# Expert weights as units of one expert's matrix in all eight pairs of a layer, instead of in the middle six

## The reference

```python
for e in range(N_EXPERTS):                      # 16
    y = (silu(hf @ w_gate[e]) * (hf @ w_up[e])) @ w_down[e]
    out = out + gates[:, e:e + 1] * y
```

## Time and profile before

| | |
|---|---|
| median of 3 runs | 698.88 us (697.13 to 699.33) |
| the profiled execution's own time | 698.79 us |
| its span from the first to the last instruction | 697.0 us |
| TensorE matmul busy | 659.8 us, 95% |
| TensorE weight load busy | 342.1 us, 49% |
| VectorE, ScalarE, GpSimd busy | 319.6, 167.1, 71.4 us |
| moved by DMA | 240.74 MB, mean 345 GB/s |
| experts of layer 0, layer 1 | about 129.7 to 340.3 us, 470.2 to 681.3 us of the span |

### The profile page before, as it was taken

The page is one execution under the profiler, slowest core; times in us unless marked ns, Lnnn a source line. Parts: engine busy times, 40 slices in busy tenths (PEclk is TensorE's granted clock), DMA queues, the critical chain, the costliest instruction groups (busy, mean ns, idle before and its releaser), DMA issues.

```text
span 697.0 us, 7595 instructions
## 1 busy us (share of the span) xinstructions
PE 659.8 (95%) x3087; PEld 342.1 (49%) x3087; DVE 319.6 (46%) x613; ACT 167.1 (24%) x324; POOL 71.4 (10%) x67
## 2 busy tenths in 40 slices
PE   7999999999999999998689999989999999999982
PEld 4874587543333543332278656856333345333330
DVE  6898867610322220320687978773220330320326
ACT  3411763231110311110153128424101113101100
POOL 3403100510000000000060040006000000000001
PEclk9999999999999999999879999999999999999996
DMA  8999836099999999999999953334999999999991
GB/s 282 367 391 414 372 123 241 13 371 395 430 428 428 428 429 427 428 422 420 394 381 403 414 228 121 122 121 194 361 420 431 427 426 430 424 432 423 420 375 63
DMA packets 39438, 240.74 MB, mean 345 GB/s; under 512 B 4508, under 2 KB 8932, under 8 KB 24036
## 3 DMA queue, kind: packets, MB, share of 16 engines
q1 hardware_dynamic: 36612, 236.49, 83.7%
q10 hardware_dynamic: 2784, 3.67, 1.5%
HBM read 239.10 MB, written 1.05 MB: 345 GB/s over the span
## 4 chain that ended last, share of the span: by engine, by line
PE 73%; DVE 11%; DMA 10%; ACT 2%; issue 2%; SPq 1%; POOL 0%; DVEq 0%; POOLq 0%; ACTq 0%
PE bank L586 22%; PE bank L619 10%; DMA ring<-in_w_up 8%; PE bank L490 8%; PE bank L504 6%; PE bank L564 5%; PE bank L601 5%; PE bank L634 4%; PE bank L654 4%; DVE mix L1435 4%; PE bank L696 2%; DMA ring<-in_w_in 2%; DVE in_lo L1212 2%; PE bank L609 1%; PE bank L768 1%
## 5 line engine op out<-in xcount | busy, mean ns | idle before, releaser
L586 PE MATMUL bank<-ring,xe 128*64 128x512 f32 x768 | 167.6, 593 | 0.1
L1372 DVE TENSOR_TENSOR area_b<-area_b,bank 128x512 f32<-128x512 f32 x16 | 11.0, 688 | 231.4 <-PE bank L586 167.0
L586 PEld LDWEIGHTS bank<-ring,xe 128*64 128x64 f32 x768 | 55.2, 137 | 108.3 <-issue 107.7
L619 PE MATMUL bank<-ring,area_b 128*64 128x512 f32 x384 | 85.0, 596 | 0.0
L1392 DVE SCALAR_TENSOR_TENSOR y_lo<-bank,slot_gate,y_hi 128x512 fp32r<-128x512 f32 x32 | 24.0, 751 | 89.4 <-ACT y_hi L959 89.4
L1060 POOL TENSOR_TENSOR rstd<-var_eps,half_neg 128x1 f32<-128x1 f32 x18 | 11.8, 659 | 512.4 <-DVE var_eps L1159 512.3
L601 PE MATMUL bank<-ring,xe 128*64 128x512 f32 x256 | 57.0, 596 | 3.7 <-DMA ring<-in_w_up 2.6
L490 PE MATMUL bank<-ring,xT_area 128*128 128x512 f32 x128 | 55.9, 593 | 0.0
L619 PEld LDWEIGHTS bank<-ring,area_b 128*64 128x64 f32 x384 | 26.5, 137 | 50.0 <-issue 50.0
L1435 DVE SCALAR_TENSOR_TENSOR mix<-mix,tapsT 128x256 f32<-128x256 f32 x120 | 49.9, 486 | 0.0
L959 ACT ACTIVATE y_hi<-bank,slot_gate 128x512 fp32r<-128x512 f32 x32 | 22.0, 687 | 98.4 <-PE bank L619 70.7
(11 more groups left out here) (171 smaller groups left out, 859.4 us busy)
## 6 DMA issues: line engine op xcount, KB each, us to landing
ring<-in_w_gate SPq DMA_DIRECT2D x32, 2048.0 KB, 20.0
ring<-in_w_up SPq DMA_DIRECT2D x32, 2048.0 KB, 19.6
ring<-in_w_down SPq DMA_DIRECT2D x32, 2048.0 KB, 21.0
ring<-in_w_in SPq DMA_DIRECT2D x9, 2048.0 KB, 18.1
ring<-in_w_out SPq DMA_DIRECT2D x4, 2048.0 KB, 21.0
ring<-in_w_in SPq DMA_DIRECT2D x2, 1024.0 KB, 7.7
h<-in_x SPq DMA_DIRECT2D x2, 512.0 KB, 4.1
ln_par<-in_ln_mix_g ACTq DMA_DIRECT2D x2, 512.0 KB, 14.7
```

The costliest lines, as they stand in the source:

```text
L586: mm = pe.matmul(bank[2 + m][e * SLOTS:(e + 1) * SLOTS, :], xe[:, k, at + e * SLOTS:at + (e + 1) * SLOTS], w[e][:, k * DE:(k + 1) * DE], s ...
L619: mm = pe.matmul(bank[5 + n][e * SLOTS:(e + 1) * SLOTS, :], hidT[:, k, e * SLOTS:(e + 1) * SLOTS], w[e][:, k * D + n * BANK:k * D + (n + 1 ...
```

## The change

The pairs 0 and 7 of each layer get the layout that pairs 1 to 6 have. The constant is the whole diff; the three engines that test it follow.

```diff
@@ -52,7 +52,7 @@
 SLABS = 5 + 2
 PAIR_UNITS = 6
 LAYER_UNITS = SLABS + PAIR_UNITS * PAIRS
-WHOLE = (1, 2, 3, 4, 5, 6)
+WHOLE = (0, 1, 2, 3, 4, 5, 6, 7)
 SLAB_COLS = [2048, 0, 512, 1536, 1024]
```

## The result

| | before | after |
|---|---|---|
| median of the timed runs | 698.0 us (4 runs) | 722.69 us (4 runs) |
| ratio, with its 95% interval | | 1.0354 (1.0335 to 1.0374) |
| span of the profiled execution | 697.0 us | 721.0 us |
| TensorE matmul busy | 659.8 us, 95% | 663.1 us, 92% |

The account below looks back on a forecast made before the run. Loads, near 427 GB/s and unbroken from about 190 us, set the end of each layer, with TensorE also near full. Waits of 12.6 us plus 3.4 for the clock, on 698.9, gave 714.9 us; range 705 to 720.

Parts of the forecast that it names:

- The price of the lines: Row length of loads: whole units gain pair 7 0.5 us per layer; pair 0's loads land early in either layout.
- Pair 0: slots come free later: Pair 0: first refill issued at 145.9 instead of 137.9; TensorE's own time there unchanged, only loads suffer.
- Late slots: Pair 0's slots freed later: loads through pair 2 delayed 3.6 us in layer 0, 3.2 in layer 1.
- single issues into a nearly empty queue cost 4.4 us in pauses: Refill through pair 2 before the change: 4.4 us of pauses, expected to vanish when loads are issued in twos.
- The pairing of pair 7: Pair 7's products wait for two units, down wholly behind its last: 2.9 us per layer taken alone.
- The shorter landings of pair 7: Pair 7's six whole units land every 4.89 us instead of 4.98, gaining 0.5 us per layer.
- The clock: Waits of about 3 us in pairs 6 and 7 each lower TensorE's clock: 1.7 us per layer, 3.4 in all.
- Rival A: Pairs 6 and 7: waits of 3 us don't lower TensorE's clock; 711.5 us, chance 0.20.
- B: Pair 0's lateness is made up, only pair 7's pairing remains: 704.7 us, 708.1 with lowered clock; chance 0.12.
- C: Refill pauses stay in part, about 1.5 us at each of two refills per layer: 721 us, chance 0.11.
- D: Not slower: long rows move much faster, needing 550 GB/s in pair 7; chance 0.07 together with the unknown.

Follow-up runs that it names:

- the hold: Changed kernel, but layer 0's pair 0 loads are issued only once ScalarE's four small loads have landed: 716.58 us, ratio 1.0258.
- the shorter rows: Changed kernel, but layer 0's pair 0 units are each loaded by two 1 MB loads with rows of 8 KB: 716.06 us, ratio 1.0246.
- A better split: Kernel before with pair 1 split as well (whole: pairs 2 to 6): 695.33 us, ratio 0.9959; with pair 2 split too: 696.38 us, ratio 0.9983.

## Why the prediction was wrong, point by point

- **The step that failed** is in "The price of the lines": "Pair 0's loads land long before use in either layout", and, from it, in "Pair 0: slots come free later": "so only the loads suffer". With them the time ahead of pair 0 went into the sum as nothing, without a word on the mixer. The weights do land early. But the loads share the DMA engines with ScalarE's small ones, whose 2.2 us of waiting before were visible at the norm, and longer rows take more of every turn. It cost 6.9 us in layer 0, and the two experiments that take it away (the hold, the shorter rows) put pair 0 back at 129.7 and 129.9. The forecast asked what the new rows do for the loads that have them, and not what they do to the queue beside them. With 6.9 us added the forecast would have been 721.8, 0.9 below the measured 722.7; that it is so near is luck, since the experts lost 3.2 us more than forecast and the stretch between the layers gave 2.0 back. Layer 1 has no such loss, and its small loads aren't on the chain there.
- **Late slots: the mechanism right, a term too small.** The issues went out when forecast, and the eight steps had no pauses. The first load landed after 8.8 us, not 8.0, and layer 1's pair 2 was 4.3 us late instead of 3.2. Alone this edit costs 4.8 and 4.7 us in the experts, where the forecast's delay of the loads was 3.6 and 3.2. The reading that failed is "single issues into a nearly empty queue cost 4.4 us in pauses": 1.5 of the 4.4 us were no pause. With loads in twos the long steps went, and the first load was 0.8 us longer.
- **The pairing of pair 7: right,** 3.3 us for each layer by itself, forecast 2.9.
- **The shorter landings of pair 7: right,** 4.90 us for a unit, 0.4 to 0.5 us for a layer.
- **The clock: right in size, wrong in rule.** It fell before pair 7's up in both layers and cost 1.7 and 1.5 us (8.75 and 8.62 us instead of 7.08), near the 3.4 us of the forecast. But not behind each wait: in those before pair 6's up and pair 7's gate it stayed. Over all profiled executions here, 13 of 32 waits of 2.4 to 2.8 us in the experts were followed by a fall, none behind a shorter one. So neither "each such wait lowers it" nor the prediction's reading that the 3.4 us were due by a rule comes out of the traces. And a fall costs only where it is not covered: with pair 7 alone changed it fell behind the wait before gate in layer 0 and not at all in layer 1, and the experts took 213.9 and 214.4 us. In the two runs with shorter rows, whose pairs run as in the changed kernel, it fell behind an earlier wait in both layers, and the experts took 218.8 to 219.0 us instead of 220.5. So the size came out right by luck. Rival A was wrong for this kernel's profile, and is as good as the forecast for any single wait.
- **Not forecast, and with the other sign:** the 2.0 us between the layers. TensorE was at 1.2 GHz for 6.9 us there instead of 13.7, so L696 took 14.1 us instead of 15.8. Over the profiled executions that time at 1.2 GHz lasted from 6.8 to 17.1 us and the stretch took 127.9 to 134.7 us; the kernel before has executions of both kinds too (see "A better split"). So this gain can't be put down to the change.
- Rivals B, C and D fell: the lateness was not made up, the two pauses went, and a long-row unit takes 4.9 us. C's 721 us lie nearer to the result than the forecast, but not for C's reason.

## What to carry to other kernels

Where loads set the end and nothing in between leaves their queue empty, a slot that comes free late costs its lateness at the end, and a product that waits for two units has all its work behind the second. When the shape of a large transfer changes, look for the small transfers on other queues at the same moment: the longer its rows, the longer each of theirs waits. Split units belong to the pair whose slots refill an empty queue and to the pair that ends last; long rows belong in the middle, where they gain a little (4.9 instead of 5.0 us for a unit).

## What the runs showed of the hardware that was not expected

- A load of 128 KB in rows of 1 KB beside a busy queue of 2 MB loads: 1.6, 2.8 and 5.3 us from the last one's landing beside rows of 4, 8 and 16 KB (3.1 beside the 8 KB rows of the kernel before), while the two queues moved one row each in turn. With the other queue empty it took 2.9 to 3.8 us from issue to landing.
- One packet of 16 KB on the instruction queue occupied one DMA engine for about 1.0 us. Of two 2 MB loads issued 0.4 us apart into an empty queue, the first landed after 8.8 us in layer 0 of the changed kernel, with such a packet in flight, and after 7.4 and 7.7 us in layer 1 of the two runs with filling matmuls, where the packet came before the load's own; there a later step between landings was 1.5 and 1.0 us longer. A link is likely and not tested.
- TensorE's clock fell behind 13 of 32 equal waits of 2.4 to 2.8 us, in different ones in the two layers and in different kernels, and was back 3.4 us later where dense work followed.
